# A two-layer hybrid decoder trunk on one core: block products with seven instead of eight multiplications for five of the eleven down units of each feed-forward

## The chip, the cores and the metric

The kernel runs on one core of a Trainium2 chip. The metric is the device time of one execution in microseconds. The kernel before took 1093.26 us (median of three runs, 1092.75 to 1097.58). The engines are named as the profile names them: PE is TensorE (PEld its weight loads), DVE is VectorE, ACT is ScalarE, POOL is GpSimd, SP is SyncE, which here only starts the weight transfers.

## The reference

The trunk has two layers, a sequence of 256 tokens and a model width of 1024, all in float32. Each layer is

```python
x = x + 0.5 * swiglu(rms_norm(x, norm_w[l, 0]), ...)
x = x + mixer(rms_norm(x, norm_w[l, 1]), ...)      # layer 0: attention and gated delta rule; layer 1: spatial gating
x = x + 0.5 * swiglu(rms_norm(x, norm_w[l, 2]), ...)

def swiglu(h, w_gate, w_up, w_down):               # 1024 -> 2816 -> 1024
    return (jax.nn.silu(h @ w_gate) * (h @ w_up)) @ w_down
```

so there are four feed-forwards, numbered f = 0 to 3 below, and the change is in those four.

## The kernel before

**Units.** All large weights are cut into units of at most 128 x 2048 values. A feed-forward has 33: for each of eleven column pairs c a gate unit (2c) and an up unit (2c+1), each 8 x 128 rows by 256 columns, and then eleven down units (22 to 32; the text calls them down unit 0 to 10), each two blocks of 128 rows by 1024 columns. Unit j lives in slot j % 4 of three rings: `raw` (as loaded), `whi` and `wlo`. SP's queue loads the raw slots in order, and the load of unit j waits until the low part of unit j-4 is there (`lo_ready`).

**Splitting.** Every product is made in float32r with a high and a low part of both operands, so that one block product is three matmuls: high by high, high by low, low by high. `hi(j)` (L466) is an ACT copy raw -> whi; it waits for the load and until PE has done unit j-4 (`unit_done`). `lo(j)` (L884) is a DVE subtraction raw - whi -> wlo. Both engines work strictly in the order in which their program is written.

**Gate and up stage.** `blocks` (its matmuls stand at L1341 to L1343) makes one gate or up unit: 2 x 8 blocks, three matmuls of 256 columns each, the weights being stationary. For pair c, DVE scales the gate sums by the row of 1/rms (`scale_gate`, L910), ACT applies silu (L511), DVE multiplies with the up sums (`product`, L919), ACT copies the high part into hTh (L517), and DVE makes the low part hTl (L926). The up sums are not scaled; the factor 1/rms of the up side comes in at the end, in `half_rstd`.

**Down stage.** `down` makes, for each down unit, 2 (row blocks k) x 2 (token blocks t) x 2 (column halves n) products of 128 x 128 by 128 x 512, that is 24 matmuls (L1382, L1383, L1386), into four PSUM banks `D_BANK`. The last two down units are not done one after the other but quarter by quarter (L1341 to L1343 with hTh as input): the sum of quarter 0 (token block 0, columns 0 to 511) is finished for both units, then quarter 1 and so on. After each quarter DVE adds it to X (`x_update`, L934), and behind quarter 1 PE transposes the updated quarter 0 for the next stage (`x_quarter`, L1429), and so on. Meanwhile ACT and DVE run `hi` and `lo` of the units ahead in a plain list (units 26 to 34, where 33 and 34 are the first two of the next stage).

The change touches `ffn` on ACT, on DVE and on PE (in this order in the file), `scale_gate`, `product`, `spread_diag`, `r_spread`, `r_sums` and `down`.

Of the kernel before, what the change touches and what calls it, by code (L numbers as in the profile page):

```python
# [5 lines left out]
P = 128  # L6
D_MODEL, SEQ, D_FF = 1024, 256, 2816
NT = SEQ // P
# [19 lines left out]
LEVELS = (2, 4, 8, 16, 32)  # L28
PAIRS_F = D_FF // 256


# [42 lines left out]
def build_trunk(nc, x, positions, norm_w, w_gate, w_up, w_down, ab_in, q_norm, w_q_b, kv_norm, w_kv_b,  # L74
# [72 lines left out]
    with ctx:  # L147
# [25 lines left out]
        H1 = KF * SEQ  # L173
        XT0 = 2 * H1
        R0 = XT0 + 2 * KD * SEQ
        arena = sb("arena", [P, R0 + 8544])

        def at(off, *dims):
            n = int(np.prod(dims))
            v = arena[:, off:off + n]  # L180
            if len(dims) == 2:
                v = v.rearrange("p (a b) -> p a b", b=dims[1])
            if len(dims) == 3:
                v = v.rearrange("p (a b c) -> p a b c", b=dims[1], c=dims[2])
            return v

        cursor = [0]
# [29 lines left out]
        r_diag = at(R0 + 2656, NT, P)  # L217
        squares = [at(R0, 1024), at(R0 + 1024, 1024)]
        wsT = at(4096, GROUPS, P)
        V = at(R0 + 4096, NT, SGW)  # L220
# [32 lines left out]

        sumsq4, sumsq, rstd, half_rstd = tiny(NT, 2), tiny(2), tiny(2), tiny(2)
        rs_a, rs_t, rs_y = tiny(32), tiny(32), tiny(32)
# [119 lines left out]
        def _(pool):  # L375
# [57 lines left out]
            pool.wait_ge(S("pv_sums"), HEADS)  # L433
            per_head(kbe, QKVn[1], begc).then_inc(S("kbe_ready"), 1)
            per_head(qd.rearrange("p t n -> p (t n)"), QKVn[0], egc).then_inc(S("qd_ready"), 1)
            per_head(kt, QKVn[1], ek).then_inc(S("kt_ready"), 1)
            pool.wait_ge(S("z_silu"), 1)
# [17 lines left out]
        def _(act):  # L455
# [39 lines left out]
            def r_spread(s):  # L495

                act.wait_ge(S("r_sums"), s + 1)
                A(r_row, B[4][:, 0:SEQ], ACT.Copy).then_inc(S("r_row_ready"), 1)

# [13 lines left out]
            def prod_hi(f, c):  # L513
# [4 lines left out]
                  ).then_inc(S("prod_hi"), 1)  # L518

            def ffn(f):  # L520
                s, base = FFN_SUB[f], u_ffn[f]
                hi(base + 2)
                hi(base + 3)
                r_spread(R_OF[s])
                if f == 0:
                    act.wait_ge(S("param_sums"), 1)
                    A(param_cols[:, 48:N_ROWS], B[3][:, 0:N_ROWS - 48], ACT.Copy).then_inc(S("params_ready"), 1)
# [60 lines left out]
            act.wait_ge(S("gate_exps"), 3)  # L588
            A(gc, gc, ACT.Ln, bias=1.0).then_inc(S("gate_ln"), 1)

# [100 lines left out]
            for h in range(HEADS):  # L691
# [21 lines left out]
                if h == 1:  # L713
                    act.wait_ge(S("dec_diff"), 1)
                    A(Dec, Dec, ACT.Exp, scale=-1.0).then_inc(S("dec_exp"), 1)
                if 1 <= h <= 4:
# [20 lines left out]
            for n in range(5):  # L737
# [4 lines left out]
                if n == 4:  # L742
                    act.wait_ge(S("qd_ready"), 1)
                    AT_out(0)
# [103 lines left out]
        def _(dve):  # L848
# [56 lines left out]
            def scale_gate(f, c):  # L905

                dve.wait_ge(S("unit_done"), u_ffn[f] + 2 * c + 1)
                if c == 0:
                    dve.wait_ge(S("r_row_ready"), R_OF[FFN_SUB[f]] + 1)
                TT(gate[:, c % 2, :].rearrange("p (b n) -> p b n", n=SEQ),  # L910
                   B[PAIR_BANK[c][0]][:].rearrange("p (b n) -> p b n", n=SEQ),
                   bc(r_row.unsqueeze(1), [P, 2, SEQ]), ALU.mult).then_inc(S("gate_scaled"), 1)

            def product(f, c):

                n = PAIRS_F * f + c
                dve.wait_ge(S("unit_done"), u_ffn[f] + 2 * c + 2)
                dve.wait_ge(S("silu_done"), n + 1)
                TT(prod[:, c % 2, :], B[PAIR_BANK[c][1]][:], gate[:, c % 2, :], ALU.mult  # L919
                   ).then_inc(S("prod_ready"), 1)  # L920

            def prod_lo(f, c):
# [3 lines left out]
                TT(hTl[:, 2 * c:2 * c + 2, :], prod[:, c % 2, :].rearrange("p (b n) -> p b n", n=SEQ),  # L926
                   hTh[:, 2 * c:2 * c + 2, :].bitcast(f32), ALU.subtract).then_inc(S("prod_lo"), 1)

            def x_update(s, q, factor):
# [17 lines left out]
            def spread_diag(s):  # L947

                dve.wait_ge(S("rstd_ready"), s + 1)
                for t in range(NT):  # L950
                    TS(r_diag[:, t, :], ident, rstd[:, t:t + 1], None, ALU.mult).then_inc(S("r_diag_ready"), 1)

# [105 lines left out]
            conv(0)  # L1058
            dve.wait_ge(S("gate_ln"), 1)
            link(STT(sp, sp, 0.0, gc, ALU.max, ALU.add))  # L1060
# [88 lines left out]

            head_norm(QKVn[1], 1, 1.0).then_inc(S("k_normed"), 1)  # L1150
            row_max(2)
# [26 lines left out]
            for h in range(HEADS):  # L1178
                if 0 < h < HEADS - 2:
                    row_max(h + 2)  # L1180
                if h == 0:
                    head_norm(QKVn[0], 0, float(DK) ** -0.5).then_inc(S("q_normed"), 1)
                if h == 1:
# [6 lines left out]
                if h == 2:  # L1190
                    dve.wait_ge(S("decay_exps"), 2)
                    link(TT(begc, beta, egc, ALU.mult))
                    dve.wait_ge(S("dec_exp"), 1)
                    TT(m3(DecB), m3(Dec), bc(beta.rearrange("p t h -> p (t h)").unsqueeze(2), [P, M, 64]), ALU.mult
# [142 lines left out]
        def _(pe):  # L1337
# [14 lines left out]
            def gemm(j, banks, k0, k_all, srcs, xi=None):  # L1352
# [14 lines left out]
                last.then_inc(S("unit_done"), 1)  # L1367

            def down(stage, base, n_units, done_before=0, upto=None, hidden=None, fresh=None):
# [110 lines left out]
            def r_sums(s):  # L1480

                pe.wait_ge(S("r_diag_ready"), 2 * s + 2)
                for t in range(NT):
                    last = mm(B[4][:, P * t:P * t + P], ones128, r_diag[:, t, :], start=True, stop=True)
                last.then_inc(S("r_sums"), 1)
# [210 lines left out]
            def head_transposes(i):  # L1696

                src, g = (QKVn[1], QKVn[0])[i // 2], i % 2
                pe.wait_ge(*((S("k_normed"), 1) if i < 2 else (S("q_normed"), 1)))
                if i:  # L1700
# [166 lines left out]

            pe.wait_ge(S("kbe_ready"), 1)
            for t in range(NT):
# [8 lines left out]

            pe.wait_ge(S("qd_ready"), 1)
            pe.wait_ge(S("early_added"), 2)  # L1880
# [21 lines left out]
            pe.wait_ge(S("qdT_out"), 2)  # L1902
            pe.wait_ge(S("kt_ready"), 1)
            for n in range(4):
# [113 lines left out]
```

## Time and profile before

| | |
|---|---|
| median of three runs | 1093.26 us (1092.75 to 1097.58) |
| the profiled execution, first to last instruction | 1094.6 us (of this execution no time outside the span is given) |
| PE busy | 1070.2 us, 98% |
| PE weight loads busy | 972.7 us, 89% |
| DVE busy | 637.0 us, 58% |
| ACT busy | 513.2 us, 47% |
| POOL busy | 49.9 us, 5% |
| mean granted TensorE clock | 0.993 |
| DMA | 184.88 MB, mean 169 GB/s |

A busy share is taken over all stages. Matmuls are pipelined, and their printed durations overlap: the pace of a run of matmuls is the distance of their starts. Idle time of an engine is printed with what released it, as `<-ACT whi L466`.

### The profile page before, as it was taken

The numbers are of one execution on the slowest core, as the hardware profiler recorded it, in microseconds if no ns is written. First come the engines' busy times: TensorE is split into PE (matmuls) and PEld (weight loads), VectorE is DVE, ScalarE is ACT, GpSimd is POOL, SyncE is SP. The second block draws the span as 40 slices with busy tenths as digits, with TensorE's granted clock in tenths as the row PEclk, the third lists the DMA queues.
The fourth block names the chain that finished last, engine by engine and source line by source line (L and its number), as shares of the span: only waits on it lengthen the run. The fifth ranks groups of instructions, "written<-read, shape, count | busy, mean of one in ns | idle before, by whom it ended". The sixth has DMA issues, their size and how long they took to land.

```text
span 1094.6 us, 18956 instructions
## 1 busy us (share of the span) xinstructions
PE 1070.2 (98%) x8393; PEld 972.7 (89%) x8393; DVE 637.0 (58%) x783; ACT 513.2 (47%) x617; POOL 49.9 (5%) x32
## 2 busy tenths in 40 slices
PE   7999999999889999999999999999999999999998
PEld 7999988998778799998889999888788889999986
DVE  5755543699853585655447555445765647555542
ACT  6644433685673354444345444334565436444430
POOL 1000000110171000000000000001000000000000
PEclk9999999999998999999999999999999999999999
DMA  9855555253004275555537665554554475555531
GB/s 308 275 180 189 193 192 180 87 193 116 1 4 156 77 231 180 179 182 191 192 116 234 191 193 191 183 177 161 180 176 183 156 228 180 185 179 189 192 115 39
DMA packets 127194, 184.88 MB, mean 169 GB/s; under 512 B 4205, under 2 KB 101722, under 8 KB 126986
## 3 DMA queue, kind: packets, MB, share of 16 engines
q1 hardware_dynamic: 126368, 181.85, 51.2%
q0 software_dynamic: 448, 1.71, 0.5%
q8 instruction: 66, 1.08, 0.4%
q10 hardware_dynamic: 298, 0.12, 0.0%
q14 instruction: 14, 0.11, 0.0%
HBM read 182.62 MB, written 1.05 MB: 168 GB/s over the span
## 4 chain that ended last, share of the span: by engine, by line
PE 92%; DVE 3%; issue 2%; ACT 1%; DMA 1%; POOLq 0%; SPq 0%; POOL 0%; ACTq 0%; DVEq 0%
PE banks L1341 21%; PE banks L1342 20%; PE banks L1343 20%; PE banks L1382 7%; PE banks L1386 7%; PE banks L1383 7%; PE banks L1739 1%; PE banks L1465 1%; PE banks L1466 1%; PE banks L1467 1%; DVE wlo L884 1%; DMA raw<-in_ffn_w_up 1%; PE banks L1429 1%; PE banks L1962 1%; PE banks L1928 0%
## 5 line engine op out<-in xcount | busy, mean ns | idle before, releaser
L884 DVE TENSOR_TENSOR wlo<-raw,whi 128x2048 fp32r<-128x2048 f32 (+1 forms) x167 | 383.5, 2302 | 228.6 <-ACT whi L466 228.5
L466 ACT ACTIVATE whi<-raw 128x2048 fp32r<-128x2048 f32 (+1 forms) x171 | 324.1, 1907 | 381.1 <-PE banks L1343 240.6
L1341 PE MATMUL banks<-xTh,whi 128*128 128x256 f32 x1408 | 396.9, 282 | 1.2 <-DVE wlo L1006 0.9
L1342 PE MATMUL banks<-xTl,whi 128*128 128x256 f32 x1408 | 395.8, 281 | 0.0
L1343 PE MATMUL banks<-xTh,wlo 128*128 128x256 f32 x1408 | 395.8, 281 | 0.0
L1341 PEld LDWEIGHTS banks<-xTh,whi 128*128 128x128 f32 x1408 | 265.6, 189 | 2.4 <-issue 1.6
L1342 PEld LDWEIGHTS banks<-xTl,whi 128*128 128x128 f32 x1408 | 265.7, 189 | 0.0
L1343 PEld LDWEIGHTS banks<-xTh,wlo 128*128 128x128 f32 x1408 | 265.6, 189 | 0.0
L1382 PE MATMUL banks<-whi,hTh 128*128 128x512 f32 x336 | 133.1, 396 | 0.0
L1383 PE MATMUL banks<-wlo,hTh 128*128 128x512 f32 x336 | 132.4, 394 | 0.0
L1386 PE MATMUL banks<-whi,hTl 128*128 128x512 f32 x336 | 105.5, 395 | 0.0
L1386 PEld LDWEIGHTS banks<-whi,hTl 128*128 128x128 f32 x336 | 63.0, 187 | 15.4
L1382 PEld LDWEIGHTS banks<-whi,hTh 128*128 128x128 f32 x336 | 63.0, 187 | 15.3
L1383 PEld LDWEIGHTS banks<-wlo,hTh 128*128 128x128 f32 x336 | 63.0, 187 | 15.0
L1341 PE MATMUL banks<-whi,xTh 128*128 128x512 f32 (+1 forms) x160 | 64.0, 400 | 0.0
L1342 PE MATMUL banks<-wlo,xTh 128*128 128x512 f32 (+1 forms) x160 | 62.7, 392 | 0.0
L1343 PE MATMUL banks<-whi,xTl 128*128 128x512 f32 (+1 forms) x160 | 62.6, 391 | 0.0
L919 DVE TENSOR_TENSOR arena<-banks,arena 128x512 f32<-128x512 f32 x44 | 30.4, 691 | 53.0 <-PE banks L1343 53.0
L1341 PE MATMUL banks<-whi,hTh 128*128 128x512 f32 (+1 forms) x120 | 50.4, 420 | 0.0
L1342 PE MATMUL banks<-wlo,hTh 128*128 128x512 f32 (+1 forms) x120 | 48.0, 400 | 0.0
L1343 PE MATMUL banks<-whi,hTl 128*128 128x512 f32 (+1 forms) x120 | 48.0, 400 | 0.0
L910 DVE TENSOR_TENSOR arena<-banks,arena 128x512 f32<-128x512 f32 x44 | 30.3, 690 | 26.9 <-PE banks L1343 26.9
(248 smaller groups left out, 994.9 us busy)
## 6 DMA issues: line engine op xcount, KB each, us to landing
raw<-in_ffn_w_up SPq DMA_DIRECT2D x44, 1024.0 KB, 5.4
raw<-in_ffn_w_down SPq DMA_DIRECT2D x44, 1024.0 KB, 4.9
raw<-in_ffn_w_gate SPq DMA_DIRECT2D x43, 1024.0 KB, 5.4
raw<-in_sg_w_in SPq DMA_DIRECT2D x16, 1024.0 KB, 5.5
raw<-in_ab_w_in SPq DMA_DIRECT2D x8, 1024.0 KB, 5.1
raw<-in_sg_w_out SPq DMA_DIRECT2D x8, 1024.0 KB, 5.0
raw<-in_ab_w_out SPq DMA_DIRECT2D x4, 1024.0 KB, 4.9
raw<-in_ab_w_in SPq DMA_DIRECT2D x2, 832.0 KB, 4.4
```

What stands on the lines that cost most here:

```text
L466: A(whi[:, j % SLOTS, 0:kt * width], raw[:, j % SLOTS, 0:kt * width], ACT.Copy).then_inc(S("hi_ready"), 1)
L884: TT(wlo[:, j % SLOTS, 0:n], raw[:, j % SLOTS, 0:n], whi[:, j % SLOTS, 0:n].bitcast(f32), ALU.subtract).then_inc(S("lo_ready"), 1)
L910: TT(gate[:, c % 2, :].rearrange("p (b n) -> p b n", n=SEQ), B[PAIR_BANK[c][0]][:].rearrange("p (b n) -> p b n", n=SEQ), bc(r_row.unsqueez ...
L919: TT(prod[:, c % 2, :], B[PAIR_BANK[c][1]][:], gate[:, c % 2, :], ALU.mult).then_inc(S("prod_ready"), 1)
L1341: mm(out_ap, lh, rh, start=first, stop=False)
L1342: mm(out_ap, lh, rl, start=False, stop=False)
L1343: return mm(out_ap, ll, rh, start=False, stop=last)
L1382: mm(o, hTh[:, kk, tok], wh[:, k, c], start=kk == 0, stop=False)
L1383: mm(o, hTh[:, kk, tok], wl[:, k, c], start=False, stop=False)
L1386: last = mm(o, hTl[:, kk, tok], wh[:, k, c], start=False, stop=False)
L1429: last = transpose(B[X_BANK[k // 2]][:, 256 * (k % 2) + P * t:256 * (k % 2) + P * t + P], X[:, t, P * k:P * k + P], ident)
L1465: mm(out_ap, lh, rh, start=first, stop=False, skip_group_check=True)
```

## The change

Down units 2 to 6 of each feed-forward (`SEVEN`, so N7 = 5) are made with seven block products instead of eight, by Winograd's form of Strassen's scheme. With the left blocks a (hidden values, two row blocks by two token blocks) and the right blocks b (weights, two row blocks by two column halves) it needs three further sums of right blocks, one sum that replaces the fourth right block, and four sums of left blocks. Down units 0 and 1, and 7 to 10, stay as they were.

- Left side (DVE and ACT, in the gate and up stage, for pairs c = 2 to 6): `left_sums` is three DVE subtractions (256, 128 and 128 columns), `sums_hi` an ACT copy of 512 columns, and `left_lo` a DVE subtraction of 512 columns one pair later.
- Since the sums mix token blocks, the hidden values have to carry the whole scale: `scale_up` is a DVE multiplication of 512 columns in every pair, and the factor at the end is 0.5.
- Right side (in the down stage, for each of the five units): `right_sums` is three DVE additions (1024, 512 and 512 columns), the last of them into raw; then `hi` on ACT (2048 columns) and a copy of the three other sums (1536 columns) on ACT; then `lo` (2048 columns) and `right_lo` (1536 columns) on DVE. There are two sets of buffers for the sums (`T_SUM`, `T_HI`, `T_LO`).
- The high and low parts of units 24 and 25 (down units 2 and 3) were made within pair 10 before; now all the down units from 2 on follow behind the last pair.
- PE: `seven_products` has 21 matmuls; four of its seven sums go to banks 0 to 3, three into the usual banks.
- `seven_added`, on DVE between `lo` of units 33 and 34: seven operations that bring banks 0 to 3 into X, with an ACT copy of bank 0 ahead of them.
- Several semaphores are merged under one name (`gate_exps`, `decay_exps`, `scaled_heads`, `heads_normed`) with the counts fitted; r_row and r_diag of the feed-forwards lie in another place (`f_row`, `f_diag`).

The diff without the merged semaphores and the buffer addresses:

```diff
             def ffn(f):                                  # ACT
...
                 for c in range(PAIRS_F):
-                    hi(base + 2 * c + 4)
+                    if c < PAIRS_F - 1:
+                        hi(base + 2 * c + 4)
                     silu_gate(f, c)
-                    hi(base + 2 * c + 5)
+                    if c < PAIRS_F - 1:
+                        hi(base + 2 * c + 5)
                     prod_hi(f, c)
-                for j in range(26, 35):
-                    hi(base + j)
+                    if c in SEVEN:
+                        sums_hi(f, SEVEN.index(c))
+                for i in range(2, 13):
+                    if i in SEVEN:
+                        k = SEVEN.index(i)
+                        act.wait_ge(S("summed"), 2 * N7 * f + N7 + k + 1)
+                        hi(base + 22 + i)
+                        A(T_HI[k % 2], T_SUM[k % 2], ACT.Copy).then_inc(S("sums_hi"), 1)
+                    else:
+                        hi(base + 22 + i)
+                    if i == 11:
+                        act.wait_ge(S("seven_sums"), 4 * f + 1)
+                        A(V1, B[0][:], ACT.Copy).then_inc(S("p1_out"), 1)
...
+            def scale_up(f, c):                          # DVE
+                dve.wait_ge(S("silu_done"), PAIRS_F * f + c + 1)
+                g = gate[:, c % 2, :].rearrange("p (b n) -> p b n", n=SEQ)
+                link(TT(g, g, bc(f_row.unsqueeze(1), [P, 2, SEQ]), ALU.mult))
...
+            def left_sums(c, k):
+                a = prod[:, c % 2, :].rearrange("p (b n) -> p b n", n=P)
+                d = S_SUM[k].rearrange("p (b n) -> p b n", n=P)
+                link(TT(d[:, 0:2, :], bc(a[:, 3:4, :], [P, 2, P]), a[:, 1:3, :], ALU.subtract))
+                link(TT(d[:, 2, :], a[:, 2, :], d[:, 0, :], ALU.subtract))
+                TT(d[:, 3, :], a[:, 0, :], d[:, 2, :], ALU.subtract).then_inc(S("summed"), 1)
+            def left_lo(f, k):
+                dve.wait_ge(S("sums_hi"), 2 * N7 * f + k + 1)
+                TT(S_LO[k], S_SUM[k], S_HI[k].bitcast(f32), ALU.subtract).then_inc(S("sums_lo"), 1)
+            def right_sums(f, k):
+                j = u_ffn[f] + 22 + SEVEN[k]
+                dve.wait_ge(S(f"raw_loaded{j % SLOTS}"), 16 * arrivals[j])
+                dve.wait_ge(S("unit_done"), u_ffn[f] + (22 if k < 2 else 23 + SEVEN[k - 2]))
+                b = raw[:, j % SLOTS, :].rearrange("p (b n) -> p b n", n=512)
+                t3 = T_SUM[k % 2].rearrange("p (b n) -> p b n", n=512)
+                link(TT(t3[:, 0:2, :], b[:, 1:3, :], bc(b[:, 3:4, :], [P, 2, 512]), ALU.add))
+                link(TT(t3[:, 2, :], t3[:, 1, :], b[:, 1, :], ALU.add))
+                TT(b[:, 3, :], t3[:, 2, :], b[:, 0, :], ALU.add).then_inc(S("summed"), 1)
+            def right_lo(f, k):
+                dve.wait_ge(S("sums_hi"), 2 * N7 * f + N7 + k + 1)
+                TT(T_LO[k % 2], T_SUM[k % 2], T_HI[k % 2].bitcast(f32), ALU.subtract).then_inc(S("sums_lo"), 1)
+            def seven_added(f):
+                c0, c1 = slice(0, 512), slice(512, 1024)
+                dve.wait_ge(S("p1_out"), f + 1)
+                STT(X[:, 0, c0], V1, 0.5, X[:, 0, c0], ALU.mult, ALU.add)
+                dve.wait_ge(S("seven_sums"), 4 * f + 2)
+                link(TT(V2, B[1][:], V1, ALU.subtract))
+                dve.wait_ge(S("seven_sums"), 4 * f + 4)
+                links[0] += 1
+                STT(X[:, 1, c1], B[3][:], 0.5, X[:, 1, c1], ALU.mult, ALU.add).then_inc(S("dve_chain"), 1)
+                link(TT(V34, banks[:, 2:4, :], bc(V2.unsqueeze(1), [P, 2, 512]), ALU.add))
+                STT(X[:, 1, c0], V34[:, 0, :], -0.5, X[:, 1, c0], ALU.mult, ALU.add)
+                STT(X[:, 1, c1], V34[:, 0, :], 0.5, X[:, 1, c1], ALU.mult, ALU.add)
+                links[0] += 1
+                STT(X[:, 0, c1], V34[:, 1, :], 0.5, X[:, 0, c1], ALU.mult, ALU.add).then_inc(S("dve_chain"), 1)
+                dve.wait_ge(S("dve_chain"), links[0])
...
                 lo(base + 2)
-                link(TS(half_rstd, rstd, 0.5, None, ALU.mult))
                 lo(base + 3)
...
                 for c in range(PAIRS_F):
                     scale_gate(f, c)
-                    lo(base + 2 * c + 4)
+                    if c < PAIRS_F - 1:
+                        lo(base + 2 * c + 4)
+                    scale_up(f, c)
                     product(f, c)
-                    lo(base + 2 * c + 5)
+                    if c < PAIRS_F - 1:
+                        lo(base + 2 * c + 5)
                     prod_lo(f, c)
-                for j in range(26, 35):
-                    lo(base + j)
-                factor = [half_rstd[:, t:t + 1] for t in range(NT)]
+                    if c - 1 in SEVEN:
+                        left_lo(f, SEVEN.index(c - 1))
+                    if c in SEVEN:
+                        left_sums(c, SEVEN.index(c))
+                for i in range(2, 11):
+                    if i in SEVEN:
+                        right_sums(f, SEVEN.index(i))
+                        lo(base + 22 + i)
+                        right_lo(f, SEVEN.index(i))
+                    else:
+                        lo(base + 22 + i)
+                lo(base + 33)
+                seven_added(f)
+                lo(base + 34)
+                factor = [0.5, 0.5]
...
+            def seven_products(base, f, k):              # PE
+                i = SEVEN[k]
+                j = base + i
+                begin(j)
+                pe.wait_ge(S("sums_lo"), 2 * N7 * f + N7 + k + 1)
+                pe.wait_ge(S("prod_lo"), PAIRS_F * f + i + 1)
+                if k == 0:
+                    pe.wait_ge(S("prod_ready"), PAIRS_F * (f + 1))
...
+                for lh, rh, bank in products:
+                    own = bank < 4
+                    last = split_mm(B[bank][:], lh[0], lh[1], rh[0], rh[1], own and k == 0, own and k == N7 - 1)
+                    if own and k == N7 - 1:
+                        last.then_inc(S("seven_sums"), 1)
+                last.then_inc(S("unit_done"), 1)
...
                 for i in range(done_before, n_units - 2 if upto is None else upto):
                     j = base + i
+                    if hidden is not None and i in SEVEN:
+                        seven_products(base, hidden // PAIRS_F, SEVEN.index(i))
+                        continue
                     wh, wl = slot(j)
```

## Rows read from the trace of the kernel before

**Rows 1.** The page: span, and the chain that ended last, by engine and by line
```profile
span 1094.6 us, 18956 instructions
PE 92%; DVE 3%; issue 2%; ACT 1%; DMA 1%; POOLq 0%; SPq 0%; POOL 0%; ACTq 0%; DVEq 0%
```
**Rows 2.** The waits: who waited for whom, us in total, times, longest us
```profile
DVE wlo L884 <- ACT whi L466: 228.5, 122, 3.6
ACT whi L466 <- PE banks L1386: 135.8, 38, 4.0
```
**Rows 3.** Groups by line and shape: count | busy us, mean ns | idle before them
```profile
L884 DVE TENSOR_TENSOR wlo<-raw,whi 128x2048 fp32r<-128x2048 f32 x163 | 376.6, 2317 | 222.0 <-ACT whi L466 221.9
L466 ACT ACTIVATE whi<-raw 128x2048 fp32r<-128x2048 f32 x167 | 318.4, 1918 | 373.5 <-PE banks L1343 240.6 <-PE banks L1386 128.2 <-DMA raw<-in_ffn_w_up 4.7
...
L926 DVE TENSOR_TENSOR hTl<-arena,hTh 128x512 fp32r<-128x512 f32 x44 | 30.1, 684 | 0.0
...
L517 ACT ACTIVATE hTh<-arena 128x512 fp32r<-128x512 f32 x44 | 27.0, 614 | 1.4 <-DVE arena L919 1.4
...
L1322 DVE TENSOR_TENSOR arena<-arena 128x1024 f32<-128x1024 f32 x4 | 4.9, 1225 | 17.4 <-ACT arena L832 17.4
```
**Rows 4.** The down stage's matmuls: shortest, median, longest ns; first and last start
```profile
L1382 PE MATMUL banks<-whi,hTh x336: 392/396/476, 138.2 to 1079.1; 128*128 128x512 f32 x168
```
**Rows 5.** ACT in the down stage of f = 0: start, duration, instruction [idle before]
```profile
144.04 1.92 ACT L466 ACTIVATE whi<-raw 128x2048 fp32r<-128x2048 f32 x1 [3.16 <-PE banks L1386]
...
183.24 1.65 ACT L466 ACTIVATE whi<-raw 128x1728 fp32r<-128x1728 f32 x1 [3.68 <-PE banks L1386]
```
**Rows 6.** DVE, f = 0: last pairs, start and end of the down stage; chained small operations
```profile
129.04 2.29 DVE L884 TENSOR_TENSOR wlo<-raw,whi 128x2048 fp32r<-128x2048 f32 x1 [1.32 <-ACT whi L466]
131.25 0.69 DVE L926 TENSOR_TENSOR hTl<-arena,hTh 128x512 fp32r<-128x512 f32 x1
...
138.39 0.69 DVE L919 TENSOR_TENSOR arena<-banks,arena 128x512 f32<-128x512 f32 x1 [1.37 <-PE banks L1343]
...
190.52 1.96 DVE L884 TENSOR_TENSOR wlo<-raw,whi 128x1728 fp32r<-128x1728 f32 x1 [3.64 <-ACT whi L466]
192.40 0.74 DVE L934 SCALAR_TENSOR_TENSOR X<-banks,small,X 128x512 f32<-128x512 f32 x1
...
207.16 0.16 DVE L868 TENSOR_TENSOR small<-small 128x2 f32<-128x2 f32 x1
207.35 0.16 DVE L869 TENSOR_TENSOR small<-small 128x2 f32<-128x2 f32 x1
```
**Rows 7.** PE, f = 0: transposes of quarter 0, behind quarter 1
```profile
194.18 0.60 PE L1429 MATMUL banks<-C,X 128*128 128x128 f32 x4
```
**Rows 8.** PE behind a wait in the first mixer's last quarters; 512-column matmuls behind it
```profile
369.17 0.66 PE L1429 MATMUL banks<-C,X 128*128 128x128 f32 x4 [1.83 <-DVE X L934]
...
370.39 0.63 PE L1343 MATMUL banks<-whi,hTl 128*128 128x512 f32 x1
370.81 0.63 PE L1341 MATMUL banks<-whi,hTh 128*128 128x512 f32 x1
...
373.31 0.40 PE L1341 MATMUL banks<-whi,hTh 128*128 128x512 f32 x1
```
**Rows 9.** PE behind its longest wait in the first mixer
```profile
279.08 0.55 PE L1770 MATMUL banks<-C,arena 128*128 128x128 f32 x3 [3.10 <-ACT arena L680]
```
**Rows 10.** By window: length, busy us of PE, PEld, DVE, ACT, POOL, then PEclk, DMA share, GB/s
```profile
18.30:138.10 119.80, 119.80 (x1013) 119.58 (x1012) 76.74 (x79) 57.78 (x50) 0.96 (x1) 1.00 0.68 216
138.10:188.50 50.40, 50.40 (x219) 40.54 (x218) 21.59 (x11) 17.50 (x10) 0.00 (x0) 1.00 0.56 183
...
279.00:280.00 1.00, 0.92 (x8) 0.93 (x9) 0.84 (x5) 1.00 (x6) 0.00 (x0) 1.00 0.00 0
...
370.00:371.00 1.00, 1.00 (x4) 0.81 (x3) 0.00 (x0) 0.49 (x2) 0.00 (x0) 0.50 1.09 378
```
**Rows 11.** DMA issues of the page: KB each, median us from issue to landing
```profile
raw<-in_ffn_w_down SPq DMA_DIRECT2D x44, 1024.0 KB, 4.9
```

More of the change, by code:

```diff
@@ L29 @@
 PAIRS_F = D_FF // 256
+SEVEN = (2, 3, 4, 5, 6)
+N7 = len(SEVEN)
 def constants():
@@ L174, in build_trunk @@
         XT0 = 2 * H1
+        with ExitStack() as over:
+            over.enter_context(nc.sbuf_tensor("hT_again", [P, XT0], f32r))
+            rounded = over.enter_context(nc.sbuf_tensor("rounded", [P, 2 * KD * SEQ + 8544], f32r))
         R0 = XT0 + 2 * KD * SEQ
@@ L185, in at, with at_r @@
             return v
+        def at_r(off, n):
+            return rounded[:, off - XT0:off - XT0 + n]
         cursor = [0]
@@ L218, in build_trunk @@
         squares = [at(R0, 1024), at(R0 + 1024, 1024)]
+        f_row, f_diag = at(R0, SEQ), at(R0 + SEQ, NT, P)
+        S_AT = [R0 + o for o in (512, 1536, 2560, 6144, 7168)]
+        S_SUM = [at(o + 512, 512) for o in S_AT]
+        S_HI, S_LO = [at_r(o, 512) for o in S_AT], [at_r(o + 512, 512) for o in S_AT]
+        T_AT = [XT0 + 3072, XT0 + 1536]
+        T_SUM, T_HI, T_LO = [at(o, 1536) for o in T_AT], [at_r(o, 1536) for o in (R0 + 4096, XT0)], [at_r(o, 1536) for o in T_AT]
+        V1, V2, V34 = at(XT0 + 1536, 512), at(XT0, 512), at(XT0 + 512, 2, 512)
         wsT = at(4096, GROUPS, P)
@@ L252, in build_trunk @@
         s_dec = at(3584, PAIRS, 64)
-        sumsq4, sumsq, rstd, half_rstd = tiny(NT, 2), tiny(2), tiny(2), tiny(2)
+        sumsq4, sumsq, rstd = tiny(NT, 2), tiny(2), tiny(2)
         rs_a, rs_t, rs_y = tiny(32), tiny(32), tiny(32)
@@ L497, in r_spread @@
                 act.wait_ge(S("r_sums"), s + 1)
-                A(r_row, B[4][:, 0:SEQ], ACT.Copy).then_inc(S("r_row_ready"), 1)
+                A(r_row if s == R_OF[1] else f_row, B[4][:, 0:SEQ], ACT.Copy).then_inc(S("r_row_ready"), 1)
             def sg_hT_hi(c):
@@ L518, in prod_hi, with sums_hi @@
                   ).then_inc(S("prod_hi"), 1)
+            def sums_hi(f, k):
+                act.wait_ge(S("summed"), 2 * N7 * f + k + 1)
+                A(S_HI[k], S_SUM[k], ACT.Copy).then_inc(S("sums_hi"), 1)
             def ffn(f):
@@ L526, in ffn @@
                     act.wait_ge(S("param_sums"), 1)
-                    A(param_cols[:, 48:N_ROWS], B[3][:, 0:N_ROWS - 48], ACT.Copy).then_inc(S("params_ready"), 1)
+                    A(param_cols[:, 48:N_ROWS], B[3][:, 0:N_ROWS - 48], ACT.Copy)
                     act.wait_ge(S("angles"), 1)
@@ L588, in _ @@
             act.wait_ge(S("gate_exps"), 3)
-            A(gc, gc, ACT.Ln, bias=1.0).then_inc(S("gate_ln"), 1)
+            A(gc, gc, ACT.Ln, bias=1.0).then_inc(S("gate_exps"), 1)
             def tap(i):
@@ L714, in _ @@
                     act.wait_ge(S("dec_diff"), 1)
-                    A(Dec, Dec, ACT.Exp, scale=-1.0).then_inc(S("dec_exp"), 1)
+                    A(Dec, Dec, ACT.Exp, scale=-1.0).then_inc(S("decay_exps"), 1)
                 if 1 <= h <= 4:
@@ L911, in scale_gate @@
                    B[PAIR_BANK[c][0]][:].rearrange("p (b n) -> p b n", n=SEQ),
-                   bc(r_row.unsqueeze(1), [P, 2, SEQ]), ALU.mult).then_inc(S("gate_scaled"), 1)
+                   bc(f_row.unsqueeze(1), [P, 2, SEQ]), ALU.mult).then_inc(S("gate_scaled"), 1)
+            def scale_up(f, c):
+                dve.wait_ge(S("silu_done"), PAIRS_F * f + c + 1)
+                g = gate[:, c % 2, :].rearrange("p (b n) -> p b n", n=SEQ)
+                link(TT(g, g, bc(f_row.unsqueeze(1), [P, 2, SEQ]), ALU.mult))
             def product(f, c):
@@ L1483, in r_sums @@
                 for t in range(NT):
-                    last = mm(B[4][:, P * t:P * t + P], ones128, r_diag[:, t, :], start=True, stop=True)
+                    last = mm(B[4][:, P * t:P * t + P], ones128, (r_diag if s == R_OF[1] else f_diag)[:, t, :], start=True, stop=True)
                 last.then_inc(S("r_sums"), 1)
```

40 lines of the change are left out of this document (26 added, 14 removed).

## The prediction

> **What bounds the kernel now.** I read the chain that ended last first: 92% of it is PE, 3% DVE [rows 1]. In the down stage that is literally so: from 138.1 to 188.5 us PE is busy all the time, DVE for 21.6 of 50.4 us and ACT for 17.5 [rows 10]. The waits say the same from the other side: 38 times ACT's copy of the high part waits for PE's last matmul of a down unit, 3.6 us each time, and DVE's low part then waits for ACT [rows 2]. The timeline of ACT gives the pace: seven steps of its copies take from 144.04 to 183.24, 5.60 us each [rows 5]. A down unit has 24 matmuls, so one takes 5.60 / 24 = 0.2333 us; the 0.396 us in the group row overlap [rows 4]. So fewer matmuls do shorten this stage, as long as the two engines that prepare the weights keep up.
>
> **What PE saves.** 24 - 21 = 3 matmuls in each of 5 x 4 = 20 units: 60 x 0.2333 = **14.0 us**. A seven-product unit takes 21 x 0.2333 = 4.90 us of PE.
>
> **What the preparation of a unit costs.** Durations of tensor-tensor operations on DVE: 0.684 us for 512 columns, 1.225 for 1024, 2.29 in the timeline for 2048 (the group's mean of 2.317 has some longer ones) [rows 3, 6]. They lie on a line, so 1536 columns take about 1.76. On ACT 512 columns take 0.614 and 2048 take 1.918, so 1536 take about 1.48 [rows 3]. An operation that waits for the one before it on its own engine starts about 0.03 us after its end (0.16 long, 0.19 apart), one that doesn't starts 0.08 before its end (131.25 after 129.04 + 2.29) [rows 6]. I take 0.03 from engine to engine too.
>
> For one unit DVE's program is: three sums, low part, low part of the sums; ACT's is: high part, high part of the sums. The high part waits for the sums, the low part for the high part, and the sums of the next unit are queued behind everything on DVE. So nothing of the next unit starts early, though there are two sets of buffers. The chain of one unit, start to start:
> - right_sums: 1.225 + 0.03 + 0.684 + 0.03 + 0.684 = 2.65
> - to ACT and its copy of 2048: 0.03 + 1.92 = 1.95 (DVE idle)
> - to DVE and lo: 0.03 + 2.29 = 2.32
> - right_lo, 1536 columns: 1.76 - 0.08 = 1.68; ACT's copy of 1536 columns (1.48) lies beside lo and is hidden
> - back to the next right_sums: -0.08
>
> Sum 8.52, taken as **8.5 us per unit** against PE's 4.9. DVE alone is busy for 6.6 of it, which is already over 4.9. The waits of right_sums for PE (the unit two before) and for its load don't decide: PE is two units on by then, and a load that lands 4.9 us after its issue [rows 11] was let go three units earlier.
>
> **Placing it in time, f = 0.** PE starts the down stage at 138.2 [rows 4]. DVE's last product starts at 138.39 [rows 6] and ends at 139.08, ACT's high part of it (0.61) at 139.72, DVE's low part at 140.43. Then the first right_sums ends at 143.0, hi at 145.0, lo at 147.3, right_lo at 149.0. PE is through with down units 0 and 1 at 138.2 + 2 x 5.60 = 149.4: no wait. The next four are ready at 149.0 + 8.5 k, the fifth (k = 4) at 183.0; PE ends it at 187.9. Between them PE idles for about 3.3 to 3.6 us, four times. Before, down unit 6 ended at 138.2 + 39.2 = 177.4. The five units thus end **10.5 us later**, the saving of 3.5 us already in it; four feed-forwards give 42.
>
> **The tail.** Behind the fifth unit DVE and ACT catch up (lo 2.3 per unit against 5.6), so down units 7 and 8 and the quarters run at the old pace, 10.5 us later. The high part of unit 33, which waits for down unit 7, moves from 183.24 [rows 5] to 193.7, its low part ends at 197.4. Only then comes seven_added: five additions into X of 0.7, V2 0.69 as L919 from PSUM [rows 6], V34 1.3 (1024 columns, between 1.225 [rows 3] and 2 x 0.69), with links and overlaps about 5.3, to 202.7; then lo of unit 34 (1.96) to 204.7; then x_update of quarter 0 to 205.4. PE is at the transposes of that quarter at 194.18 + 10.5 = 204.7 [rows 7]. So it waits 0.7 us where it waits for nothing now (the update runs from 192.40 [rows 6]). In f = 1 and 2 the two units are 2048 wide instead of 1728: 2 x 0.3 more, 1.4 us each. In f = 3 no next stage is split, and the old updates end in time: 0. Sum about **3.5 us**; bounds 0 and 6.
>
> **What is hidden.** In the gate and up stage DVE gets 0.68 per pair for scale_up and, for five pairs, 0.68 (left_lo) and about 1.1 (left_sums: by the same line 0.42 for 256 columns, 0.3 twice). It had 6.7 of 11.35 us per pair, now up to 9.2. ACT gets one copy of 0.61. The next scale_gate may start 1 us late, but PE needs that bank and those weights only two to three units later. Cover: some 5 us per pair; if it were gone, up to 2 us per pair would show. I take 0. The dropped half_rstd operation (0.2 us, behind lo), merged semaphores and the moved f_row are 0: the same waits at the same places.
>
> **The clock.** A wait of PE of 1.83 us is followed by matmuls 0.63 us long and 0.42 apart (370.39 to 370.81) instead of 0.40 and 0.233, until at 373.31 the old length is back [rows 8]; the granted clock meanwhile is 0.50, the 1.2 GHz level, against 1.00 or 2.4 GHz [rows 10]. But a wait of 3.10 us at 276 to 279 left it at 1.00 [rows 9, 10]. In such a spell of 3.4 us some 8 matmuls run, each 0.19 later than at full clock: 1.6 us. Behind the first three gaps it is free, since PE has 3.6 us to spare; behind the fourth it is on the path. As the rows stand at one and one, I count it in two feed-forwards of four: **3 us**, bounds 0 and 6.5. The Trainium skill ("TensorE: Matmul & The Clock Gate", section "HAM oscillation") tells of bursts of matmuls that each start at half clock because the waits between them re-throttle the engine. By it all four would pay, which is rival 1; of the two waits above one agrees with it and one doesn't.
>
> **Sum.** 42 + 3.5 + 3 = 48.5 us more. Against the profiled execution, 1094.6 us, that is 1143.1; against the median, 1.3 us lower, 1141.8. I say **1142 us**, 4.5% slower.
>
> **Rivals.**
> 1. *The clock falls in every one of the gaps.* Each unit from the second on starts with a spell of 1.6 us of loss, and all four feed-forwards show it behind the last gap: 42 + 3.5 + 6.5 = 52, 1145 us. For it: the wait of 1.83 us. Against it: the one of 3.10 [rows 8, 9]. Chance 25%.
> 2. *The clock stays low through whole units.* 21 x 0.42 = 8.9 us per unit is more than the chain's 8.5, so PE never idles again and yet sets the pace: units k = 1 to 4 run from 157.5 to 193.1, 16 us later than before, 64 + 3.5 and some 3 for the recovery: 1163 us. For it: the spell at 0.50. Against it: that spell ended while PE was working without a break. Chance 6%.
> 3. *Preparation keeps up, and the 14 us come in.* Place: DVE's five passes per unit. It decides from a chain of 4.9 us per unit. If DVE's passes ran at twice the rate of the rows, the chain would be 3.3 + 1.95 = 5.2, nearly there, and the time about 1093.3 - 14 + 3 = 1082 us. Against it: all widths of tensor-tensor rows lie on one line [rows 3]. The Trainium skill ("VectorE: DVE Perf Modes", on the mode that uses both read ports) says that fp32 tensor_tensor can't have the double rate; these rows agree. Chance 3%.
> 4. *The chain is partly hidden*, because operations are shorter or a wait is less strict than I read it: 6.6 us per unit (DVE's own work alone, ACT's copy hidden). Then 42 shrinks to 42 - 4 x 4 x 1.9 = 12, and the time is 1093.3 + 12 + 5 = 1110. Against it: lo reads what hi writes, and hi waits for all three sums. Chance 4%.
> 5. *Slower elsewhere too*: the cover of the gate and up stage fails, 0.5 to 1 us in each of 20 to 40 pairs: 1160 to 1175. Against it: PE waits for a product two pairs back. Chance 4%.
>
> My forecast has 58%.
>
> **Range.** In the forecast the period may be off by 0.3 (16 gaps: 5 us), the tail by 3, the clock by 3.5; that makes 1131 to 1154. It takes in rival 1; stretched by a little towards rivals 2 and 4: 1130 to 1158. What a measurement can tell from no change is 0.5%, 5.5 us: slower by more than that 95%, within 2%, faster 3%.
>
> **What the changed profile should show.** PE waits for DVE's low part of the sums ahead of down units 3 to 6, sixteen waits of 2 to 4 us, none ahead of down unit 2. In that stretch DVE's right_sums start 8.5 us apart and DVE waits only for ACT, 2 us per unit. Seven-product units with 0.233 between starts, some with 0.427 at first. A wait of L1429 for X of about 1 us in f = 0 to 2. A gate and up stage that is as long as before (119.8 us in f = 0). I am wrong if PE has no such waits, or if the five units end less than 7 us later than before.

## The result, and the profile after

The changed kernel takes 1145.02 us (median of four runs, 1138.68 to 1148.61) where the kernel before, with a fourth run, takes 1093.61: the ratio is 1.0461, 95% interval 1.0425 to 1.0498. The forecast was 1142 us, 4.5% slower, in a range of 1130 to 1158.

The page of the kernel after, its span and the chain that ended last (of before: [rows 1]):

```profile
span 1143.7 us, 19136 instructions
...
PE 75%; DVE 15%; ACT 5%; issue 4%; DMA 0%; ACTq 0%; DVEq 0%
```

PE's part of the chain fell from 92% to 75%; DVE has 15% of it and ACT 5%. The waits of the kernel after (who waited for what, us in total, times, longest us) show where:

```profile
ACT whi L482 <- DVE raw L991: 97.2, 20, 5.2
...
PE banks L1441 <- issue: 43.4, 16, 3.4
PE banks L1567 <- DVE X L1020: 4.2, 4, 1.8
```

The second row is the result in one line: 16 waits of PE, four in each feed-forward, 43.4 us in total. L1441 is the first of the three matmuls of a block product, and each of the 16 that wait opens a seven-product unit. The profile puts these waits down to "issue", that is to nothing it shows, but in the timelines below PE starts 0.1 us after the end of DVE's last operation for the unit. The first row is the same chain seen from ACT: the high part of a unit waits for the last of the right sums, 20 times, 5.2 us each in the steady state, where before it waited for PE [rows 2].

DVE in the down stage of f = 0, kernel after (start, duration, operation): the end of the gate and up stage, the first unit, and the start of the second and third.

```profile
138.24 0.69 DVE L958 TENSOR_TENSOR arena<-banks,arena 128x512 f32<-128x512 f32 x1 [3.67 <-PE banks L1443]
139.63 0.69 DVE L965 TENSOR_TENSOR hTl<-arena,hTh 128x512 fp32r<-128x512 f32 x1 [0.70 <-ACT hTh L533]
140.24 1.22 DVE L989 TENSOR_TENSOR arena<-raw 128x1024 f32<-128x1024 f32 x1
141.49 0.69 DVE L990 TENSOR_TENSOR arena<-arena,raw 128x512 f32<-128x512 f32 x1
142.22 0.69 DVE L991 TENSOR_TENSOR raw<-arena,raw 128x512 f32<-128x512 f32 x1
144.89 2.29 DVE L918 TENSOR_TENSOR wlo<-raw,whi 128x2048 fp32r<-128x2048 f32 x1 [1.99 <-ACT whi L482]
147.10 1.75 DVE L996 TENSOR_TENSOR rounded<-arena,rounded 128x1536 fp32r<-128x1536 f32 x1
148.77 1.22 DVE L989 TENSOR_TENSOR arena<-raw 128x1024 f32<-128x1024 f32 x1
...
155.64 1.75 DVE L996 TENSOR_TENSOR rounded<-arena,rounded 128x1536 fp32r<-128x1536 f32 x1
157.30 1.22 DVE L989 TENSOR_TENSOR arena<-raw 128x1024 f32<-128x1024 f32 x1
...
181.22 1.75 DVE L996 TENSOR_TENSOR rounded<-arena,rounded 128x1536 fp32r<-128x1536 f32 x1
```

From one L989 to the next it is 148.77 - 140.24 = 8.53 us, and again 8.53. DVE works without a break but for the 1.99 us in which ACT makes the high part; it never waits for a weight load. The last low part of the sums (L996) ends at 182.97. PE's starts behind a wait, in the same stretch [idle before]:

```profile
157.49 0.47 PE L1441 MATMUL banks<-whi,hTh 128*128 128x512 f32 x1 [3.28 <-issue]
166.02 0.47 PE L1441 MATMUL banks<-whi,hTh 128*128 128x512 f32 x1 [3.43 <-issue]
174.55 0.48 PE L1441 MATMUL banks<-whi,hTh 128*128 128x512 f32 x1 [1.87 <-issue]
183.08 0.48 PE L1441 MATMUL banks<-whi,hTh 128*128 128x512 f32 x1 [3.43 <-issue]
```

The first of these follows 0.1 us on DVE's L996 of 155.64, which ends at 157.39. The starts are 8.53 us apart, DVE's period, and there is no wait ahead of down unit 2. The third wait is shorter because the unit before it was slower. The windows of the four units behind a wait show the clock (length, PE, PEld, DVE, ACT, POOL, PEclk, DMA share, GB/s):

```profile
157.50:162.40 4.90, 4.90 (x21) 3.82 (x21) 2.85 (x4) 2.39 (x2) 0.00 (x0) 1.00 0.49 200
166.00:170.90 4.90, 4.88 (x15) 3.90 (x15) 2.85 (x4) 2.36 (x2) 0.00 (x0) 0.65 0.50 204
174.50:179.40 4.90, 4.85 (x21) 3.87 (x21) 2.85 (x4) 2.33 (x2) 0.00 (x0) 1.00 0.50 203
183.10:189.60 6.50, 6.50 (x21) 5.14 (x22) 6.49 (x3) 2.65 (x2) 0.00 (x0) 0.74 0.90 300
```

A unit with the granted clock at 1.00 (the 2.4 GHz level) has its 21 matmuls done in 4.90 us; in a slow one the clock is 0.50 (the 1.2 GHz level) at first, as from 184.1 to 186.1 us, and back at 1.00 by 187.1, and the unit needs 6.5. Every second unit is slow: the second and fourth behind a wait in f = 0, the first and third in f = 1, 2 and 3.

The gate and up stage is as long as before, 119.8 us of PE work without a break, though DVE's part rose from 76.7 [rows 10] to 88.1 us; the window of after:

```profile
18.30:138.10 119.80, 119.80 (x1012) 119.59 (x1011) 88.12 (x107) 58.41 (x54) 0.76 (x1) 1.00 0.68 216
```

**Where the time went.** The start of DVE's last `product` in each feed-forward makes four marks. Before they lie at 138.39, 503.74, 692.50 and 1029.83, after at 138.24, 518.56, 719.50 and 1068.19, and the ends at 1094.6 and 1143.7. The shift is -0.2, 14.8, 27.0, 38.4 and 49.1, so the four feed-forwards, each with what follows it up to the next mark, add 15.0, 12.2, 11.4 and 10.7 us. Up to 291.68 us (a matmul that stood at 279.08 [rows 9]) the shift is 12.6, at 383.91 (369.17 before [rows 8]) it is 14.7: 2.1 us come in the first mixer, in which the change adds no work (it only merges semaphores there). The runs below have the same mixer code as the changed kernel, and this stretch takes between 86.6 and 92.1 us in their eight profiled executions, 90.1 in the one of before and 92.2 in the one of after. It goes with the granted clock of the stretch: 0.98 in three that take 86.6 to 87.8 us, 0.94 in before, 0.93 in after. So the 2.1 us are how this stage varies from execution to execution, and not shown to be a cost of the change.

### The profile page after: what moved, and what is told of

Same layout as the page of the kernel before. It is cut to its first block, busy times and chain, and to the rows that moved or that the text cites. A ratio compares the mean times of both kernels' runs of the same rounds, so it can differ in the third digit from the quotient of the medians.

```text
span 1143.7 us, 19136 instructions
## 1 busy us (share of the span) xinstructions
PE 1073.9 (94%) x8333; PEld 969.6 (85%) x8333; DVE 793.4 (69%) x1011; ACT 551.9 (48%) x661; POOL 46.8 (4%) x32
## 4 chain that ended last, share of the span: by engine, by line
PE 75%; DVE 15%; ACT 5%; issue 4%; DMA 0%; ACTq 0%; DVEq 0%
PE banks L1441 20%; PE banks L1443 20%; PE banks L1442 20%; DVE wlo L918 5%; ACT whi L482 4%; DVE arena L989 2%; DVE rounded L996 2%; PE banks L1520 2%; PE banks L1524 2%; PE banks L1521 2%; PE banks L1877 1%; DVE arena L990 1%; DVE raw L991 1%; PE banks L1603 1%; PE banks L1604 1%
## 5 line engine op out<-in xcount | busy, mean ns | idle before, releaser
L1441 PE MATMUL banks<-xTh,whi 128*128 128x256 f32 x1408 | 396.4, 282 | 1.8 <-DVE wlo L1106 1.6
L1441 PEld LDWEIGHTS banks<-xTh,whi 128*128 128x128 f32 x1408 | 265.3, 188 | 3.1 <-issue 2.5
L1441 PE MATMUL banks<-whi,hTh 128*128 128x512 f32 (+1 forms) x180 | 78.2, 434 | 43.4 <-issue 43.4
L1441 PEld LDWEIGHTS banks<-whi,hTh 128*128 128x128 f32 x180 | 36.1, 201 | 57.3 <-issue 49.7
L1443 PE MATMUL banks<-whi,hTl 128*128 128x512 f32 (+1 forms) x180 | 75.1, 417 | 0.0
L1442 PE MATMUL banks<-wlo,hTh 128*128 128x512 f32 (+1 forms) x180 | 74.2, 412 | 0.0
L1520 PE MATMUL banks<-whi,hTh 128*128 128x512 f32 x176 | 69.8, 397 | 0.0
L1521 PE MATMUL banks<-wlo,hTh 128*128 128x512 f32 x176 | 69.4, 394 | 0.0
L1441 PE MATMUL banks<-whi,xTh 128*128 128x512 f32 (+1 forms) x160 | 64.0, 400 | 0.1
L1524 PE MATMUL banks<-whi,hTl 128*128 128x512 f32 x176 | 55.3, 395 | 0.0
L539 ACT ACTIVATE rounded<-arena 128x512 fp32r<-128x512 f32 x20 | 12.6, 632 | 78.1 <-DVE arena L974 78.1
L958 DVE TENSOR_TENSOR arena<-banks,arena 128x512 f32<-128x512 f32 x44 | 30.4, 692 | 26.3 <-PE banks L1443 25.0
L1443 PEld LDWEIGHTS banks<-whi,hTl 128*128 128x128 f32 x180 | 35.9, 199 | 8.9
L1442 PEld LDWEIGHTS banks<-wlo,hTh 128*128 128x128 f32 x180 | 36.3, 202 | 6.9
```

What stands on the lines that cost most here:

```text
L539: A(S_HI[k], S_SUM[k], ACT.Copy).then_inc(S("sums_hi"), 1)
L1441: mm(out_ap, lh, rh, start=first, stop=False)
L1442: mm(out_ap, lh, rl, start=False, stop=False)
L1443: return mm(out_ap, ll, rh, start=False, stop=last)
L1520: mm(o, hTh[:, kk, tok], wh[:, k, c], start=kk == 0, stop=False)
L1521: mm(o, hTh[:, kk, tok], wl[:, k, c], start=False, stop=False)
```

## The experiments

The kernel before took 1093.75 us beside the first four variants below and 1093.28 beside the others; the ratios are to it, and all edits are to the changed kernel. The second and the last add matmuls for their time alone, so that their output isn't the reference's. Where texts below speak of e3 and e4, these are the overlapped order and every second unit.

### The left side alone

All down units are direct again; of the change there stay `scale_up`, the left sums and the later low parts of units 24 and 25.

```diff
-                    if hidden is not None and i in SEVEN:
-                        seven_products(base, hidden // PAIRS_F, SEVEN.index(i))
-                        continue
...
-                    if i in SEVEN:
-                        right_sums(f, SEVEN.index(i))
-                        lo(base + 22 + i)
-                        right_lo(f, SEVEN.index(i))
-                    else:
-                        lo(base + 22 + i)
+                    lo(base + 22 + i)
...
-                seven_added(f)
```

> All down units are made with eight products again; what stays of the change is the left side (scale_up in every pair, left sums with their high and low parts for five pairs), the low parts of units 24 and 25 behind the last pair, and the factor 0.5. The sums of the right side, seven_products and seven_added are gone, and nothing reads the left sums. Theory (DVE and ACT prepare the right side one unit at a time, 8.5 us per unit; the left side is hidden): as before, 1093.6 us, within 3. Rival (the left side costs time in the gate and up stage, 0.5 to 1 us per pair): 1105 or more.

Measured: 1093.17 us, ratio 0.9996 (0.9975 to 1.0016). The windows of this kernel:

```profile
18.30:138.10 119.80, 119.80 (x1012) 119.58 (x1011) 88.45 (x109) 58.77 (x54) 0.78 (x1) 1.00 0.66 217
138.10:188.50 50.40, 50.40 (x219) 40.55 (x218) 23.80 (x12) 19.31 (x11) 0.00 (x0) 1.00 0.54 183
```

PE is busy throughout in both stages. So the left side costs nothing that can be seen (the interval would hide 2.7 us): 88.4 us of DVE work fit under 119.8 us of PE. The same holds for the merged semaphores and the moved rows, which this kernel keeps. The loss comes from what it leaves out: the right side and what follows it.

### PE's saving taken away

```diff
-                    products = tuple(products[n] for n in (0, 4, 5, 6, 2, 3, 1))
+                    products = tuple(products[n] for n in (0, 4, 5, 6, 6, 2, 3, 1))
+                else:
+                    products = products + (products[6],)
```

> As the changed kernel, but each seven-product unit does one product twice (24 matmuls instead of 21), so that PE's saving is gone and the output differs. Theory (PE waits for the preparation, so its saving only shows behind the last of the five units): +0.7 us per feed-forward, 1145 + 2.8 = 1148 us, and gaps ahead of down units 3 to 6 that are 0.7 us shorter. Rival (PE's work sets the time): +14 us, 1159.

Measured: 1144.47 us, ratio 1.0447 (1.0407 to 1.0488). 60 more matmuls, 14 us of PE work, don't move the time by anything that the interval can show. The +2.8 us lie within it, so the total neither shows nor excludes them; the +14 are excluded. In the profiled executions the stretch from the second mark to the third, in which the last unit runs at full clock in both, is 201.64 us against 200.94 in the changed kernel: the +0.7. PE's starts in f = 0:

```profile
158.72 0.47 PE L1441 MATMUL banks<-whi,hTh 128*128 128x512 f32 x1 [2.58 <-issue]
167.24 0.47 PE L1441 MATMUL banks<-whi,hTh 128*128 128x512 f32 x1 [1.18 <-issue]
175.77 0.47 PE L1441 MATMUL banks<-whi,hTh 128*128 128x512 f32 x1 [2.72 <-issue]
184.30 0.47 PE L1441 MATMUL banks<-whi,hTh 128*128 128x512 f32 x1 [1.20 <-issue]
```

The period is 8.53 us as before; the longer units went into the waits, 2.58 instead of 3.28 ahead of down unit 3. (The waits of 1.18 and 1.20 stand behind slow units.)

### The same work, overlapped

```diff
                 # ACT
-                        act.wait_ge(S("summed"), 2 * N7 * f + N7 + k + 1)
-                        hi(base + 22 + i)
-                        A(T_HI[k % 2], T_SUM[k % 2], ACT.Copy).then_inc(S("sums_hi"), 1)
+                        act.wait_ge(S("t_part"), 2 * (N7 * f + k) + 1)
+                        A(T_HI[k % 2][:, 0:1024], T_SUM[k % 2][:, 0:1024], ACT.Copy)
+                        act.wait_ge(S("t_part"), 2 * (N7 * f + k) + 2)
+                        A(T_HI[k % 2][:, 1024:1536], T_SUM[k % 2][:, 1024:1536], ACT.Copy).then_inc(S("sums_hi"), 1)
+                        act.wait_ge(S("summed"), 2 * N7 * f + N7 + k + 1)
+                        hi(base + 22 + i)
...
                 # DVE (the first two additions of right_sums also count up t_part)
                         right_sums(f, SEVEN.index(i))
-                        lo(base + 22 + i)
+                        dve.wait_ge(S("summed"), 2 * N7 * f + N7 + SEVEN.index(i) + 1)
                         right_lo(f, SEVEN.index(i))
+                        lo(base + 22 + i)
```

> As the changed kernel, but ACT copies the high part of the right sums first, in two pieces that start behind the first and the second addition, and then the unit's own high part; DVE makes the low part of the sums first. The same operations in another order. Theory (the period is the chain of DVE and ACT): 2.65 (sums) + 0.3 (wait) + 1.75 (low part of the sums) + 0.1 + 2.3 (low part), so 7.1 us per unit instead of 8.53; the first unit is ready 1.4 us earlier, too, which helps as PE is not there yet: 5 x 1.4 = 7.1 us per feed-forward, 28 in all: 1117 us. Rival (DVE's amount of work or PE sets the time, not the order): unchanged, 1145.

Measured: 1116.64 us, ratio 1.0191 (1.0150 to 1.0231), 28 us less than the changed kernel. DVE's timeline:

```profile
147.91 1.22 DVE L992 TENSOR_TENSOR arena<-raw 128x1024 f32<-128x1024 f32 x1
149.16 0.69 DVE L994 TENSOR_TENSOR arena<-arena,raw 128x512 f32<-128x512 f32 x1
149.89 0.69 DVE L996 TENSOR_TENSOR raw<-arena,raw 128x512 f32<-128x512 f32 x1
150.85 1.76 DVE L1001 TENSOR_TENSOR rounded<-arena,rounded 128x1536 fp32r<-128x1536 f32 x1 [0.27 <-ACT rounded L567]
152.59 2.29 DVE L921 TENSOR_TENSOR wlo<-raw,whi 128x2048 fp32r<-128x2048 f32 x1
```

The first unit's L992 starts at 141.03, this one at 147.91: 6.88 us per unit. The same operations with the same durations (but for ACT's copy in two pieces); what changed is the wait for ACT, from 1.99 to 0.27 us. PE's waits ahead of seven-product units fell from 16 with 43.4 us to 12 with 18.1, and they are now put down to `DVE wlo L921`, the low part. What is left is DVE's own 6.6 us against PE's 4.9. That the total met the forecast of 1117 us so closely is partly luck. From the fourth mark to the end the profiled execution takes 67.6 us, against 75.5 in the changed kernel: 7.9 us for a feed-forward and not 7.1, which would make 32. But in the first three feed-forwards the last seven-product unit ran slow (granted clock 0.65 or 0.66 over its first 4.9 us), in the changed kernel only in the first.

### Every second unit

```diff
-SEVEN = (2, 3, 4, 5, 6)
+SEVEN = (2, 4, 6)
```

> As the changed kernel, but three seven-product units per feed-forward, each with a direct one behind it (down units 2, 4 and 6). Theory: a pair of units costs DVE and ACT 8.53 + 2.2 = 10.7 us and PE 4.9 + 5.6 = 10.5, so the waits of PE nearly vanish (0.3 us at most); 3 x 4 x 0.7 = 8.4 us gained, seven_added delays the updates by about 1 us in three feed-forwards: 1088 to 1090 us. Rival (a seven-product unit costs its wait wherever it stands): three fifths of the loss, 1093.6 + 31 = 1124.

Measured: 1088.67 us, ratio 0.9949 (0.9931 to 0.9967). This is faster than the kernel before, with the changed kernel's own order of preparation. PE has no wait ahead of any down unit; what stays is the wait of the transposes for X, here in f = 0 and in f = 1:

```profile
192.92 0.66 PE L1567 MATMUL banks<-C,X 128*128 128x128 f32 x4 [0.17 <-DVE X L1020]
...
555.53 0.66 PE L1567 MATMUL banks<-C,X 128*128 128x128 f32 x4 [1.10 <-DVE X L1020]
```

### seven_added earlier

```diff
                     else:
                         lo(base + 22 + i)
+                seven_added(f)
                 lo(base + 33)
-                seven_added(f)
                 # ACT: the copy of bank 0 behind unit 32 instead of 33
-                    if i == 11:
+                    if i == 10:
```

> As e4 (units 2, 4, 6, the changed kernel's own order of preparation), but seven_added ahead of the low part of unit 33. Theory: the updates of quarter 0 are no longer late, 0.2 us in the first and 1.1 us in the second and third feed-forward: 2.4 us less than e4, 1086. Rival (the delay of the update is hidden anyway): as e4, 1088.7.

Measured: 1083.87 us, ratio 0.9921 (0.9896 to 0.9945). Of PE's four waits for X (4.2 us in e4, the kernel before this one) one is left, the 1.8 us of the first mixer that stand in [rows 8]:

```profile
PE banks L1567 <- DVE X L1020: 1.8, 1, 1.8
```

The wait in f = 1 was on the path: from the second mark to the third it is 188.29 us in e4 and 186.93 here. In f = 2 it hardly was, 336.01 against 335.56 from the third to the fourth, since PE here waits 1.0 us for POOL in the second mixer, as in the kernel before, and in e4 it doesn't. The total fell by 4.8 us, more than the 2.4 that were forecast; but the two were not measured side by side and their intervals overlap, so its size stays open.

### Three units with both orders, and four

The three-unit kernel with the overlapped order as well:

> Three seven-product units (2, 4, 6), overlapped order, seven_added early. Theory: no waits of PE are left, the whole saving of 3 x 4 x 0.7 = 8.4 us is there: 1085. Rival (the direct cost of the other added work, which nothing hides, is some us): 1088 as e4.

Measured: 1084.61 us, ratio 0.9920 (0.9894 to 0.9946), the same as without the overlap. With a direct unit between, the slower order was already fast enough.

Four units:

```diff
-SEVEN = (2, 3, 4, 5, 6)
+SEVEN = (2, 3, 5, 7)
# with the overlapped order and the early seven_added
-                        act.wait_ge(S("seven_sums"), 4 * f + 1)
+                        act.wait_ge(S("seven_sums"), 4 * f + 4)
```

> Four seven-product units per feed-forward (down units 2, 3, 5 and 7), the overlapped order of preparation as in e3, and seven_added ahead of the low part of unit 33 instead of behind it. Theory: DVE needs 6.9 us for a seven-product unit and 2.2 for a direct one; with two units of lead at the start and a direct unit between, every one is ready before PE is there (154.7 against 154.3 for the second one at worst); seven_added lies in a stretch in which DVE has nothing else to do, and the update of quarter 0 is just in time. 4 x 4 x 0.7 = 11.2 us gained: 1082 to 1084. Rival (a third of the waits stays, or seven_added delays the update): 1088 or more, no better than e4.

Measured: **1081.28 us**, ratio 0.9900 (0.9870 to 0.9931): the lowest median of all, 1.0% faster than the kernel before; its interval overlaps with those of the last two kernels with three units, so that four are better than three isn't shown. The window of down units 0 to 8 in f = 0 and of the 3 us behind them:

```profile
138.10:189.00 50.90, 50.90 (x219) 40.74 (x219) 46.88 (x36) 27.24 (x21) 0.00 (x0) 1.00 0.55 185
```

PE is busy without a break and so, nearly, is DVE: 46.9 of 50.9 us. A fifth unit would add 6.6 - 2.3 = 4.3 us to DVE's work here and take 0.7 from PE's, 51.2 against 50.2 us, so I expect that it would bring waits back; that wasn't tried.

### The gaps filled

```diff
+                for _ in range(12 if k else 0):
+                    mm(B[0][:], hTh[:, 0, 0:P], hTh[:, 0:2, :], start=False, stop=False)
                 begin(j)
```

> As the changed kernel, but PE makes 12 further matmuls of 512 columns (2.8 us, into bank 0, so that the output differs) ahead of the waits of down units 3 to 6, so that it idles some 0.5 us instead of 3.4. Theory (the granted clock falls behind the long gaps, and that only shows behind the last one of each feed-forward): granted clock 1.00 in all five units, 1.6 us less wherever the last unit was slow, so 1 to 6 us less than the changed kernel: 1139 to 1144. Rival (the clock has nothing to do with the gaps): clock at 0.65 in every second unit as before, and 1145 or, where the further matmuls delay the units, more.

Measured: 1143.6 us (1142.86 to 1144.4, four runs), ratio 1.0459 (1.0424 to 1.0494). The window of units 2 to 6 in f = 0:

```profile
149.40:192.00 42.60, 39.92 (x171) 31.41 (x170) 33.75 (x25) 20.49 (x12) 0.00 (x0) 1.00 0.47 163
```

and PE's waits in the whole kernel:

```profile
PE banks L1441 <- issue: 10.8, 16, 0.7
```

With waits of at most 0.7 us the granted clock is 1.00 in all sixteen units behind a wait, where it was 0.65 in eight of them. That the long waits are what lets the clock fall in these units is thereby shown. What it costs in total (1.4 us between the medians) lies inside the intervals, but the traces place it: from the first mark to the second it is 378.6 us instead of 380.3, in the one feed-forward whose last unit had been slow, and the next three stretches are as long as in the changed kernel within 0.03 us. The four runs lie within 1.5 us of each other where the changed kernel's spread over 10; with four runs each, that alone would show little.

## Why the prediction was right

**The saving of PE** (14.0 us, 4.90 us per unit): right, and worth nothing behind a slower feeder. The units with full clock take 4.90 us, and the run with 24 matmuls is as fast.

**The chain of a unit** (8.52 us, taken as 8.5): 8.53 measured. Each term holds: 1.22, 0.69 and 0.69 for the sums, 1.99 to and through ACT, 2.29 and 1.75 for the low parts. That it is the order which makes the chain this long is shown by the run that changes only the order: 6.88 us per unit and 28 us less, at the same work.

**The place in time** (ready at 149.0, PE through at 149.4; waits of 3.3 to 3.6 us ahead of units 3 to 6, none ahead of unit 2): the waits are 3.28 and 3.43 us at full clock. The last unit starts at 183.08, forecast 183.0. 42 us for the four feed-forwards are therefore right: the shift of f = 3, where nothing else is added, is 10.7 us against 10.5. One sign was read too narrowly: sixteen waits of 2 to 4 us were forecast, and seven of the sixteen are 1.85 to 1.88, those behind slow units.

**The tail** (0.7 + 1.4 + 1.4 = 3.5 us): 0.18, 1.11 and 1.11, 2.4 in all. The updates with a constant factor take 0.69 us, not the 0.75 of [rows 6], and start 0.61 apart where nothing is waited for, so DVE is there 0.3 us earlier than I had added up, and PE comes 0.2 us later, at a shift of 10.7 instead of 10.5. Moving seven_added took these waits away.

**What is hidden** (left side 0): confirmed by the run with the left side alone, 0.9996.

**The clock** (two of four feed-forwards, 3 us): the rule "half of them" was near, the place wasn't. Every second unit was slow, but since the pattern alternates, the last one was slow only in f = 0 of the profiled execution: 1.6 us instead of 3. The Trainium skill ("TensorE: Matmul & The Clock Gate", section "HAM oscillation") tells of a kernel in which every burst of matmuls behind a wait for its data starts at half clock. The trace agrees for eight of the nine units behind waits of 3.3 to 3.4 us; the one behind the 3.28 us at 157.49 ran at full clock, and so did all seven behind the waits of 1.85 to 1.88.

**Sum.** 42 + 3.5 + 3 = 48.5 was forecast, the profiled executions differ by 49.1. By what was measured it is 4 x 10.7 (the five units) + 2.4 (tail) + 1.6 (clock) + 2.1 (the first mixer, in which I had expected nothing) - 1.0 (a wait of PE for POOL in the second mixer that before has and after doesn't) = 47.9, and 1.2 that I can't place. The sum is better than its parts: the 42 are met by the mechanism, but the tail and the clock were 2.5 us too high, and that the mixer's 2.1 make up for it is luck, since that stage is as much longer or shorter between executions of the same code. Between the medians it is 51.4.

Of the rivals, "the clock falls in every one of the gaps" and "the clock stays low through whole units" fell with the windows (1.00 in every second unit); that the first had named 1145 us, the very median, is chance, since its loss behind the last gap was there in one feed-forward and not in four. "Preparation keeps up" and "partly hidden" fell with the 43.4 us of waits, and "slower elsewhere too" with the 119.8 us of the gate and up stage. What "preparation keeps up" and "partly hidden" describe came about in the variants, though by another order or spacing and not by faster operations.

## What to carry to other kernels

A cheaper algorithm for the bounding engine pays only if its preparation fits under the shortened work: compare per unit, here 6.6 us of DVE plus 2 us of waiting for ACT against 4.9 us of PE. Before giving such an algorithm up, look at two things that need no further work of any engine: whether costly and cheap units can alternate (the same saving per unit, now with its time hidden), and whether two engines that hand one piece to and fro work on it at once or in turn. And when the bounding engine is made faster by a share of its load, the others' idle time per unit tells about how many units can be converted; here four of eleven fitted, and more with a spread-out order were not tried.

## What the runs showed of the hardware that I had not expected

The granted clock doesn't fall behind each long wait but alternates: wait of 3.4 us, slow unit (6.5 us), wait of 1.9, full unit (4.9), wait of 3.4 and so on, in all four feed-forwards. The length of the wait alone doesn't decide it: a unit ran at 1.00 behind 3.28 us (f = 0, changed kernel), and in the overlapped order the one at 175.93 us started slow behind a wait of 1.79 (0.65 over its first 4.9 us), while the one at 1078.31 ran at 1.00 behind 1.77. In none of the profiled executions do two slow ones of these units stand side by side. A slow unit takes its 1.6 us out of the wait behind it, so of the eight slow units of the profiled execution only one cost anything, the last one of f = 0. And the 16 waits that matter most carry no name in the profile of the changed kernel ("issue"), although DVE's low part of the sums released them; in the overlapped order, where `wlo` comes last, the profile names it.
